# Loading x in eight pieces of 512 columns and multiplying its first quarter before the rest is transposed, in a fused two-block transformer kernel

## What is computed

```python
def first_block(x, attn_norm, w_qkv, ...):
    h = rmsnorm(x, attn_norm[l])                       # x * rsqrt(mean(x*x) + eps) * gain, over 2048
    qkv = jnp.einsum('bsd,de->bse', h, w_qkv[l])       # [256, 2048] @ [2048, 6144]
    q_a, k_a, v_a, q_b, k_b, v_b, q_c, k_c, v_c = split_columns(qkv)
    ...                                                # three kinds of attention
    x = x + jnp.einsum('bse,ed->bsd', y, w_o[l])
    ...                                                # gated MLP of width 5632, residual, norm
def reference(...):
    return second_block(first_block(...), ...)         # latent and sparse attention, cross attention, MLP of 8192
```

## Time and profile before

| | us |
|---|---|
| median of 3 runs | 2365.74 (2364.39 to 2365.76) |
| the profiled execution | 2365.81 |
| its span in the trace | 2364.0 |
| TensorE matmul busy | 2345.7 |
| VectorE busy | 1573.5 |
| ScalarE busy | 1233.3 |

### The profile page before, as it was taken

One profiled execution on the slowest core, in us unless ns is written; L12 is line 12 of the kernel. 1 busy time (PEld: TensorE's weight loads), 2 busy tenths in 40 slices (PEclk: granted clock), 3 DMA queues, 4 the chain that ended last, 5 costly groups with the idle time before them and its releaser, 6 DMA issues.

```text
span 2364.0 us, 31610 instructions
## 1 busy us (share of the span) xinstructions
PE 2345.7 (99%) x12203; PEld 2000.7 (85%) x12203; DVE 1573.5 (67%) x2466; ACT 1233.3 (52%) x1894; POOL 5.2 (0%) x12
## 2 busy tenths in 40 slices
PE   9999999999999999999999999999999999999998
PEld 8888888888888888888887888888888888888887
DVE  6787777777777657755667655666766556556555
ACT  6566566655555435544556555556544444444443
POOL 0000000000000000000000000000000000000000
PEclk9999999999999999999999999999999999999999
DMA  7544455455555564575564545654565655665664
GB/s 242 191 159 165 141 163 161 162 207 183 179 206 186 196 194 180 179 231 187 172 199 142 186 147 154 199 180 148 180 195 192 194 190 191 193 190 187 214 195 152
DMA packets 119061, 432.11 MB, mean 183 GB/s; under 512 B 13392, under 2 KB 13664, under 8 KB 118400
## 3 DMA queue, kind: packets, MB, share of 16 engines
q1 hardware_dynamic: 117504, 424.10, 55.0%
q0 software_dynamic: 976, 5.39, 0.6%
q10 hardware_dynamic: 432, 0.60, 0.1%
HBM read 427.93 MB, written 2.11 MB: 182 GB/s over the span
## 4 chain that ended last, share of the span: by engine, by line
PE 95%; DVE 3%; ACT 1%; issue 1%; DMA 0%; SPq 0%; DVEq 0%; ACTq 0%
PE bank L497 29%; PE bank L483 15%; PE bank L485 15%; PE bank L484 15%; PE bank L511 15%; DVE lo_w L1450 1%; PE bank L561 1%; DVE xT L1619 0%; PE bank L783 0%; PE bank L911 0%; PE bank L605 0%; PE bank L627 0%; PE bank L766 0%; PE bank L591 0%; ACT hi_w L988 0%
## 5 line engine op out<-in xcount | busy, mean ns | idle before, releaser
L1450 DVE TENSOR_TENSOR lo_w<-raw_w,hi_w 128x1024 fp32r<-128x1024 f32 x804 | 964.3, 1219 | 536.6 <-ACT hi_w L988 535.4
L988 ACT ACTIVATE hi_w<-raw_w 128x1024 fp32r<-128x1024 f32 x804 | 832.6, 1052 | 585.4 <-PE bank L485 402.7
L497 PE MATMUL bank<-xT,hi_w 128*128 128x512 f32 x3008 | 724.8, 391 | 1.5 <-DVE xT L1619 1.5
L497 PEld LDWEIGHTS bank<-xT,hi_w 128*128 128x128 f32 x3008 | 551.5, 188 | 107.9 <-DVE xT L1619 1.7
L511 PEld LDWEIGHTS bank<-xT,lo_w 128*128 128x128 f32 x3008 | 387.0, 191 | 15.3 <-issue 0.3
L511 PE MATMUL bank<-xT,lo_w 128*128 128x256 f32 x3008 | 393.4, 283 | 0.1
L483 PE MATMUL bank<-hi_w,act_hi 128*128 128x512 f32 x864 | 336.4, 389 | 0.0
L485 PE MATMUL bank<-hi_w,act_lo 128*128 128x512 f32 x864 | 336.1, 389 | 0.0
L484 PE MATMUL bank<-lo_w,act_hi 128*128 128x512 f32 x864 | 336.1, 389 | 0.0
L483 PE MATMUL bank<-hi_w,xT 128*128 128x512 f32 (+1 forms) x672 | 266.0, 396 | 0.1
L485 PE MATMUL bank<-hi_w,xT 128*128 128x512 f32 (+1 forms) x672 | 261.0, 388 | 0.0
(11 more groups left out here) (339 smaller groups left out, 1597.8 us busy)
## 6 DMA issues: line engine op xcount, KB each, us to landing
raw_w<-in_w_up SPq DMA_DIRECT2D x216, 512.0 KB, 4.1
raw_w<-in_w_down SPq DMA_DIRECT2D x216, 512.0 KB, 3.6
raw_w<-in_w_gate SPq DMA_DIRECT2D x88, 512.0 KB, 3.6
raw_w<-in_w_in SPq DMA_DIRECT2D x72, 512.0 KB, 4.1
raw_w<-in_w_qk SPq DMA_DIRECT2D x64, 512.0 KB, 4.3
raw_w<-in_w_v SPq DMA_DIRECT2D x32, 512.0 KB, 3.9
raw_w<-in_w_o SPq DMA_DIRECT2D x32, 512.0 KB, 3.5
raw_w<-in_w_out SPq DMA_DIRECT2D x32, 512.0 KB, 3.7
```

The costliest lines, as they stand in the source:

```text
L497: last = e.matmul(pair[c][:, :], hi_w[:, slot, at:at + P], both[:, kt].rearrange("p h t -> p (h t)"), start=(kt == 0), stop=(kt == g.kts - ...
L988: e.activation(hi_w[:, u % SPLIT_SLOTS, 0:unit_cols[u]], raw_w[:, u % RAW_SLOTS, 0:unit_cols[u]], ACT.Copy).then_inc(s["w_hi"], 1)
L1450: e.tensor_tensor(lo, raw_w[:, u % RAW_SLOTS, 0:unit_cols[u]], hi.bitcast(F32), ALU.subtract).then_inc(s["w_lo"], 1)
```

## The change

x is loaded in eight transfers of 512 columns (256 KB each) instead of four of 1024, and a weight unit goes behind each two of them. Each piece has its own semaphores. TensorE transposes piece 0, multiplies unit 0, transposes pieces 1 and 2, multiplies unit 1, transposes piece 3, multiplies unit 2. ScalarE and VectorE split unit 1 ahead of piece 1 instead of behind it. The warming matmuls are seven instead of nine. GpSimd waits for the last of the eight transfers.

```diff
--- before.py
+++ after.py
@@ -34,7 +34,7 @@
 UNIT = 1024
 RAW_SLOTS = 4
 SPLIT_SLOTS = 4
-WARM = 9
+WARM = 7
 Q_SCALE = HD ** -0.5
 
 EXPS = "natural_log_exp_and_others"
@@ -56,7 +56,8 @@
 
 SEMAPHORES = [
     "ident_landed", "consts_landed", "first_gains_landed", "gains_landed", "rel_table_landed", "rel_ext_landed", "hankel_landed", "lams_landed",
-    "x_landed00", "x_landed01", "x_landed10", "x_landed11", "warm_cleared", "warmed",
+    "x_landed00", "x_landed01", "x_landed02", "x_landed03", "x_landed10", "x_landed11", "x_landed12", "x_landed13",
+    "warm_cleared", "warmed",
     "raw_landed0", "raw_landed1", "raw_landed2", "raw_landed3",
     "end_gain1_landed", "end_gain2_landed", "pos_landed", "mem_landed", "stored",
     "w_hi", "w_lo", "w_used", "part_out", "sum_out", "copied", "x_added", "x_gained", "x_scaled", "x_squared",
@@ -566,7 +567,7 @@
 
                 if burst == "attn":
                     for t in range(TT):
-                        e.wait_ge(s[f"x_landed{t}{piece // 2}"], 16)
+                        e.wait_ge(s[f"x_landed{t}{piece}"], 16)
                 elif burst == "mix":
                     e.wait_ge(s["x_gained"], 2 * (piece + 1))
                 else:
@@ -810,11 +811,12 @@
             last.then_inc(s["warmed"], 1)
             e.wait_ge(s["ident_landed"], 16)
             turn_x("attn", 0)
+            units(1)
             turn_x("attn", 1)
-            units(1)
             turn_x("attn", 2)
+            units(1)
             turn_x("attn", 3)
-            units(2)
+            units(1)
             e.wait_ge(s["consts_landed"], 16)
             units(3)
             spread_row("attn", TURNED0["y1"])
@@ -1251,9 +1253,9 @@
             e.wait_ge(s["first_gains_landed"], 16)
             turn_x("attn", 0)
             split_hi(0)
-            turn_x("attn", 1)
             x_squares(0)
             split_hi(1)
+            turn_x("attn", 1)
             turn_x("attn", 2)
             split_hi(2)
             turn_x("attn", 3)
@@ -1888,8 +1890,8 @@
             e.tensor_copy(lo_w[:, 3, 0:512], qkT[:, 30:32, :].rearrange("p a t -> p (a t)")).then_inc(s["warm_cleared"], 1)
             turn_x("attn", 0)
             split_lo(0)
+            split_lo(1)
             turn_x("attn", 1)
-            split_lo(1)
             turn_x("attn", 2)
             split_lo(2)
             turn_x("attn", 3)
@@ -2092,12 +2094,11 @@
                     e.dma_start(raw_w[:, u % RAW_SLOTS, 0:unit_cols[u]],
                                 unit_source(u)).then_inc(s[f"raw_landed{u % RAW_SLOTS}"], 16)
 
-            for c in range(2):
+            for piece in range(4):
                 for t in range(TT):
-                    cols = slice(1024 * c, 1024 * c + 1024)
-                    e.dma_start(x[:, t, cols], dram["x"][t * P:(t + 1) * P, cols]).then_inc(s[f"x_landed{t}{c}"], 16)
-                weights(c, c + 1)
-            weights(2, 4)
+                    cols = slice(512 * piece, 512 * piece + 512)
+                    e.dma_start(x[:, t, cols], dram["x"][t * P:(t + 1) * P, cols]).then_inc(s[f"x_landed{t}{piece}"], 16)
+                weights(piece, piece + 1)
             e.dma_start(gains[:, DK:], dram["gains"][:, DK:]).then_inc(s["gains_landed"], 16)
             e.dma_start(consts[:, P:], dram["consts"][:, P:]).then_inc(s["consts_landed"], 16)
             weights(4, n_units)
@@ -2113,7 +2114,7 @@
 
 
         def gpsimd_program(e):
-            e.wait_ge(s["x_landed11"], 16)
+            e.wait_ge(s["x_landed13"], 16)
             e.dma_start(lams[:, :, :], bass.AP(tensor=dram["lambdas"].tensor, offset=0,
                                                ap=[[0, P], [HD, 4], [1, HD]])).then_inc(s["lams_landed"], 16)
             e.dma_start(ext_sb[:, 127:319], dram["rel_rev"]).then_inc(s["rel_table_landed"], 16)
```

More of the change, by code:

```diff
@@ L812, in tensor_program @@
             turn_x("attn", 0)
+            units(1)
             turn_x("attn", 1)
+            turn_x("attn", 2)
             units(1)
-            turn_x("attn", 2)
             turn_x("attn", 3)
-            units(2)
+            units(1)
             e.wait_ge(s["consts_landed"], 16)
```

## The result

The changed kernel took 2369.09 us (median of 22 runs, 2366.33 to 2369.52), the one before in the same comparison 2365.45 (22 runs, 2364.33 to 2366.18): 3.64 us more, a ratio of 1.0015 with an interval of 1.0008 to 1.0022. The forecast was 2367.5 in a range of 2365.2 to 2370.0 and "within 0.2%"; the time lies in the range, and nearest to the rival in which the clock falls once, 2369.2. The profiled execution took 2369.33 with a span of 2367.5.

What follows compares the result with a forecast made beforehand. TensorE, busy 2345.7 of 2364.0 us, was taken as the bound, with only the first 24 us reachable. Unit 0 1.35 us earlier and a stretch to unit 3 3.1 us longer gave +1.75: 2367.5 us, range 2365.2 to 2370.0.

Steps and rivals of the forecast that it cites:

- the rival in which the clock falls once: Start of the kernel: TensorE at half clock for 3.4 us, costing 1.7 us, so 2369.2 us; chance 0.3.
- The work of order: From unit 0 to unit 3: reordering adds 3.1 us, 0.95 of moved transposes plus 1.25 and 0.9 of waiting.
- the head start: Ahead of unit 0: smaller first transfers and shorter warming let unit 0 start 1.35 us earlier.
- X: Start time of unit 0 on TensorE: forecast 9.06 us instead of 10.41, as 6.4 + 1.44 + 1.22.
- The bound that I weighed most, the gains: Before unit 0: ScalarE's first copy also waits for the first gains, between 5.95 and 7.2; middle taken, 6.4.
- the 2.34 us: In the trace before: time between identity and gains landing, said to disagree with the skill's whole-packet rule.
- The stands: TensorE standing still on the split of x or weights: 1.37 us ahead of unit 1, 0.9 ahead of unit 3.
- 13.7: Time from unit 0's start to unit 3's start in us, against 10.61 before.
- The sum: Whole kernel: -1.35 + 3.1 = +1.75 us, giving 2367.5 us.
- before's stretch from 6.0 to 10.3: Ahead of unit 0 before the change: 2.01 us of transposes in 4.3 us kept the higher clock level.
- The rival of two falls: Half clock ahead of unit 0 and again around the standing ahead of unit 1: +5.15 us, 2370.9; chance 0.06.
- the 31.9 of the text: Forecast issue time in us of the Hankel load for the flips, instead of 28.91; it lands near 42.0.

Runs made afterwards that it cites:

- The order alone: Kernel before, with its four transfers and nine warming matmuls, given the changed kernel's order on TensorE, ScalarE and VectorE: 2371.18 us, ratio 1.0021.
- the transfers alone: Changed kernel's eight transfers and seven warming matmuls, with the order of the kernel before on all three engines: 2364.61 us, ratio 0.9996.

## Why the prediction was right, point by point

The time lies in the range because the range took in one fall of the clock, which the prediction held for the less likely case. The work of order was sized right; the head start was 0.5 us too large, and the 1.6 us of the clock weren't in the sum. Both misses go the same way: no errors cancelled, and it was the width of the range that held them.

**X.** Forecast 9.06, 1.35 early; measured 9.59, 0.82 early. Two terms were mis-sized. Piece 0 was to be there before the warming ended and TensorE to start at 5.2; it waited for x until 5.73, and the chain of the changed kernel has (start, us, what)

```profile
1.18 4.42 DMA x<-in_x
```

so the second 256 KB landed at 5.60, while 512 KB in a single transfer landed at 4.54. And I took 0.73 us for the first pair, a duration at 2.4 GHz; its transposes took 1.10 in the changed kernel's trace and 0.64 where the higher level was there in time. The bound that I weighed most, the gains, did not bind: they landed 4.6 us after issue, at 5.8, where before they took 5.9, and ScalarE began at 6.92, released by TensorE. That they came 1.3 us sooner fits the reading that the two queues advance together: they landed 0.2 us behind the second transfer of x in both kernels (7.09 behind 6.89, 5.79 behind 5.60). It decided nothing. Whether the queues take turns row by row or by a whole transfer's rows at a time these landings don't show: with a turn of SyncE's queue between the identity and the gains, either would give them. So the 2.34 us don't speak, as the prediction has it, against the rule of whole packets in the Trainium skill (DMA: Bandwidth & Descriptors, Queues, rings and completion order).

**The stands.** 1.37 ahead of unit 1: measured 1.32, and 1.31 to 1.32 in every kernel with this order. 0.9 ahead of unit 3: measured 0.82, and 0 once the split went first. Transposes of piece 3 and unit 2 together take 3.81 us (20.13 to 23.94), forecast 0.95 + 2.87. From X to unit 3 I had 13.7; the trace has 15.18, of which 1.57 is unit 0 at half clock (4.42 from its start to the first transpose, for 2.85), which leaves 13.61.

**The sum.** -0.82 + 3.0 + 1.57 = 3.75. The forecast had -1.35 + 3.1 and gave the clock a chance of 0.3. (By its bounds of X the forecast's lower end is 2365.74 + 1.3 = 2367.0 and not 2366.9.) The fall came in the profiled execution, at the price given for it (1.7 forecast, 1.57 found), with nine warming matmuls too, and with the old transfers for twice as long. Of the 22 runs of the changed kernel 18 lie between 2368.7 and 2369.6 and four from 2366.3 to 2368.0, so in most it fell and in a few it may not have: the mean granted clock of the fastest was 1.000, of the 18 slower ones 0.997 or 0.998. With nine warming matmuls 3 of 11 lie as low (2367.06 to 2367.39). The odds were the wrong way round: I weighed before's stretch from 6.0 to 10.3, which had 2.01 us of matmul in it and kept its clock, as evidence against, though the new one held only 0.7 to 1 us. The rival of two falls, over 0.2% slower, came nowhere. The order alone reached its time, 2371.18, by another way: one fall of twice the length, without the head start; in no profiled execution did the clock fall at the stand ahead of unit 1.

**What cost nothing.** No transfer of x made TensorE wait behind unit 0, and up to 60 us no wait on the constants or the Hankel load appears: the flips' load was issued at 33.3 instead of 28.91, later than the 31.9 of the text since unit 3's rounding came later still, and TensorE was that much later too.

## What to carry to other kernels

Ahead of a piece of work that is started early, look at what moves behind it. Here 0.8 us of earlier start was paid with two waits on conversions (2.1 us), which had been covered as long as the next input was prepared ahead of the unit that preceded its use. A gap like the one of 2.3 us here in TensorE's stream, even where nothing else could run, can cost more again in clock, 1.6 us here: put the next transposes there, or matmuls on zeros. And a change of four parts should be run by parts: the transfers alone had a median 1.0 us under before (an interval that still holds no change), the order alone one 5.5 us above.

## What was not expected of the hardware

Two transfers of 256 KB, issued 0.43 us apart, had both landed 1.1 us later than one of 512 KB issued at the first one's time (5.60 against 4.54). The 1.1 is of this one pair of traces: in the others the second of the two landed from about 5.2 on, and the single one from about 4.3. The order of the two is the same in all. Eight matmuls on zeros, work that was added ahead of unit 0, went with a median 2.0 us lower, somewhat more than the 1.2 to 1.7 that was expected. And the half-clock stretch was 3.4 us long in the changed kernel and about 6.8 with the order alone (by the clock of the windows from 7 to 24 us), under gaps of nearly the same length, 2.29 and 2.32 us. It also began sooner, at about 9.1 in the gap itself instead of 10.2 in unit 0. The order alone has 1.06 us of idle ahead of its eight transposes too, where the changed kernel has 0.47; whether that is the reason, no run shows.
